# Two slabs side by side behind each norm, factors moved to the copy out of the banks, and products for two tiles

## The reference, cut to what matters

```python
mod = silu(c) @ w_mod + b_mod
sh1, sc1, g1, sh2, sc2, g2 = split(mod, 6)
h = rmsnorm(x, attn_norm_g) * (1 + sc1) + sh1        # "h4"
proj = h @ w_in                                      # 1856 columns: qa (1024), ka, cq, ckv
...                                                  # two kinds of attention
x = x + g1 * (mix @ w_out)
h = rmsnorm(x, mlp_norm_g) * (1 + sc2) + sh2         # "h6"
u = relu(h @ w_ff1)                                  # 8192 columns
x = x + g2 * ((u * u) @ w_ff2)
return rmsnorm(x, final_norm_g)
```

## Time and profile before

| | |
|---|---|
| median of 3 runs | 2221.35 us (2219.59 to 2227.68) |
| the profiled execution | 2218.01 us |
| its span in the trace | 2216.2 us |
| granted TensorE clock, mean | 0.988 |
| busy: PE / DVE / ACT | 2136.4 / 1507.9 / 1056.5 us |
| the last product before the first norm; the first behind it | 1207.70; 1214.86 us |
| the first two slabs behind the first norm end | 1248.58 us |
| the last product before the second norm; the first behind it | 1486.16; 1493.01 us |
| the first two slabs behind the second norm end | 1525.5 us |

### The profile page before, as it was taken

How to read it: one execution, slowest core, us unless ns; L and a number is a source line. 1 busy time by engine, 2 the same in 40 slices (tenths; PEclk the granted TensorE clock), 3 DMA queues, 4 the chain that set the end, 5 groups by cost and what they waited for, 6 DMA issues and landing times. The chain is left out here.

```text
span 2216.2 us, 29175 instructions
## 1 busy us (share of the span) xinstructions
PE 2136.4 (96%) x11414; PEld 1841.3 (83%) x11414; DVE 1507.9 (68%) x1919; ACT 1056.5 (48%) x1501; POOL 50.5 (2%) x51
## 2 busy tenths in 40 slices
PE   6999999999999999999998799998999999999998
PEld 5888888888888888888877698877888888888886
DVE  5967676789798777978955566556655566556655
ACT  4644554454444434444444556545443344334443
POOL 3200000000000000000000000000000000000000
PEclk9999999999999999999999999999999999999999
DMA  7787333779698897878955324354555555555553
GB/s 259 281 298 258 131 134 115 268 286 335 249 337 308 295 350 271 335 270 320 336 205 200 131 89 145 134 209 152 190 190 193 190 190 189 192 198 191 189 181 131
DMA packets 71047, 494.44 MB, mean 223 GB/s; under 512 B 8090, under 2 KB 8394, under 8 KB 13184
## 3 DMA queue, kind: packets, MB, share of 16 engines
q1 hardware_dynamic: 67968, 480.54, 60.0%
q0 software_dynamic: 2368, 11.32, 1.5%
q10 hardware_dynamic: 576, 0.73, 0.1%
HBM read 490.40 MB, written 2.16 MB: 222 GB/s over the span
## 5 line engine op out<-in xcount | busy, mean ns | idle before, releaser
L1657 DVE TENSOR_TENSOR m_WLO<-m_RAW,m_WHI 128x1024 fp32r<-128x1024 f32 (+1 forms) x728 | 880.9, 1222 | 539.4 <-ACT m_WHI L1329 527.2
L1329 ACT ACTIVATE m_WHI<-m_RAW 128x1024 fp32r<-128x1024 f32 (+1 forms) x728 | 753.8, 1045 | 748.3 <-PE region L974 388.2
L918 PE MATMUL region<-m_HL,m_WHI 128*128 128x512 f32 x1568 | 385.3, 396 | 1.4 <-ACT m_vw L1258 1.4
L974 PE MATMUL region<-m_WHI,m_HL 128*128 128x512 f32 x1152 | 361.8, 395 | 1.2 <-DVE m_HL L1845 0.5
L918 PEld LDWEIGHTS region<-m_HL,m_WHI 128*128 128x128 f32 x1568 | 289.3, 190 | 57.4 <-ACT m_vw L1258 1.8
L918 PE MATMUL region<-m_H,m_WHI 128*128 128x512 f32 x1376 | 332.6, 393 | 0.0
L918 PEld LDWEIGHTS region<-m_H,m_WHI 128*128 128x128 f32 x1376 | 254.6, 190 | 49.4
L974 PEld LDWEIGHTS region<-m_WHI,m_HL 128*128 128x128 f32 x1152 | 212.2, 188 | 43.3 <-issue 1.4
L974 PE MATMUL region<-m_WLO,m_HL 128*128 128x512 f32 x576 | 224.7, 390 | 0.0
L1710 DVE SCALAR_TENSOR_TENSOR m_ACC<-m_RAW,m_cact,m_ACC 128x2048 f32<-128x2048 f32 x90 | 211.2, 2346 | 1.8 <-DMA m_RAW<-in_w_mod 1.8
L922 PE MATMUL region<-m_HL,m_WLO 128*128 128x256 f32 x1568 | 208.8, 285 | 0.1
(11 more groups left out here) (296 smaller groups left out, 1787.5 us busy)
## 6 DMA issues: line engine op xcount, KB each, us to landing
m_RAW<-in_w_ff SPq DMA_DIRECT2D x128, 1024.0 KB, 4.8
m_RAW<-in_w_mod SPq DMA_DIRECT2D x96, 1024.0 KB, 5.8
m_RAW<-in_ffn_w_in SPq DMA_DIRECT2D x88, 1024.0 KB, 6.0
m_RAW<-in_ffn_w_out SPq DMA_DIRECT2D x44, 1024.0 KB, 6.4
m_RAW<-in_nsa_w_in SPq DMA_DIRECT2D x40, 1024.0 KB, 5.6
m_RAW<-in_nsa_w_out SPq DMA_DIRECT2D x16, 1024.0 KB, 5.0
m_RAW<-in_w_out SPq DMA_DIRECT2D x16, 1024.0 KB, 4.9
m_RAW<-in_w_in SPq DMA_DIRECT2D x10, 1024.0 KB, 4.7
```

The source lines that it names most:

```text
L918: mm = e.matmul(region[s["reg"]][:, b, :], hi[:, i, c:c + 128], both[:, k + a + i, :, :].rearrange("p a s -> p (a s)"), start=k + a + i == ...
L974: mm = e.matmul(o, lhs, rhs, start=start and i == 0, stop=fin and i == 2, skip_group_check=True)
L1329: e.activation(WHI[u % 4][:, 0:(z - a) * ncol], raw[:, a * ncol:z * ncol], ACT.Copy).then_inc(a_hi, 1)
L1657: e.tensor_tensor(WLO[u % 4][:, 0:m], raw[:, a * ncol:z * ncol], WHI[u % 4][:, 0:m].bitcast(F32), ALU.subtract).then_inc(v_lo, 1)
```

## The change

1. **Two slabs side by side.** qa 0 and qa 1, and relu 0 and relu 1, get chunks of four k tiles (`per=4`, 512 KB, parts of two k tiles: 128 x 512) and are queued alternately: four k tiles of the first (A), the same four of the second (B), the next four of A, and so on. Neither is `by_part` now.
2. **When the norms are put.** `x_ready` puts norms 0 to 3 before k tile 0 of A, and then two at a time: 4 and 5 before A's k tile 2, 6 and 7 before B's k tile 2, 8 and 9 before A's k tile 6, 10 and 11 before B's k tile 6, and so on.
3. **Factors at the copy out.** ACT's copies from banks 4 and 5 to `XGT` become four of 128 x 256 with the factor as scale, where there were two of 128 x 512. The factors are computed when their columns of `mod` are there (unit `factors`).
4. **Products for two tiles.** `HT = XGT * root` is now a `tensor_tensor`, for tiles 0 and 1 one at a time with the root read from bank 6, and from tile 2 on for two tiles at once (128 x 512) from `rstd`. ACT's copy of the root (`rowkeep`) stands behind norm 1, its copy of the last four turned tiles (`turnout`) behind norm 3. Of the unit norm 2, `LO[1]` comes before the product.
5. The four `final` units are put at every third tick, with a rate of one.

```diff
-    for s in (sl_qa[0], sl_qa[1], sl_ka, sl_qa[2], sl_qa[3], sl_cq, sl_ckv):
+    queue(sl_qa[0], sl_qa[1])
+    for s in (sl_ka, sl_qa[2], sl_qa[3], sl_cq, sl_ckv):
         queue(s)
...
+        if pi == 0:
+            queue(up[0], up[1])
+        for s in up[2 if pi == 0 else 0:]:
             queue(s)
...
-            s["by_part"] = s["x"] in seen
+            s["by_part"] = s["x"] in seen and s["list"][0][2] == 8
...
+            if p in (1, 4):
+                put("factors", p // 4)
...
-            while normed[x] < min(KT, k + 9):
+            c, second = k // 4 * 4, s["arg"] == 1
+            while normed[x] < (min(KT, c + 4 + 2 * second + (2 if k % 4 >= 2 else 0)) if s["arg"] < 2 else KT):
                 put("norm", x, normed[x])
                 normed[x] += 1
+                if normed[x] == 2:
+                    put("rowkeep", 2 if x == "h4" else 3)
+                if normed[x] == 4:
+                    put("turnout", x, 12)
...
-        put("turnout", which, 12)
         st["owed"] = 2
...
-    side.extend(("final", m0) for m0 in range(0, KT, 4))
+    for m0 in range(0, KT, 4):
+        side.extend([None, None, ("final", m0)])
+    st["rate"] = 1
...
-                    for b in range(2):
-                        e.activation(XGT[:, m0 + 2 * b:m0 + 2 * b + 2, :], two(bank[4 + b]), ACT.Copy).then_inc(b_out[4 + b], 1)
-            elif name == "rowcast":
+                    w.wait_ge(v_gates, 1 if which == "h4" else 2)
+                    g = G1c if which == "h4" else G2c
+                    for i in range(4):
+                        m = m0 + i
+                        ins = e.activation(XGT[:, m, :], two(bank[4 + i // 2])[:, i % 2, :], ACT.Copy, scale=g[:, m:m + 1])
+                        if i % 2:
+                            ins.then_inc(b_out[4 + i // 2], 1)
+            elif name == "rowkeep":
                 r, = arg
                 w.wait_ge(p_row, r)
+                if r > 1:
+                    w.wait_ge(v_ht, product_no("h4" if r == 2 else "h6", 1))
                 e.activation(rstd[:, :], bank[6][:, 0:S], ACT.Copy).then_inc(b_out[6], 1)
...
-                e.scalar_tensor_tensor(HT[m % 8 // 4][:, m % 4, :], XGT[:, m, :], g[:, m:m + 1], rstd[:, :],
-                                       ALU.mult, ALU.mult).then_inc(v_ht, 1)
-                if m > 0:
+                if m == 1 or m % 2 == 0:
+                    n = 1 if m < 2 else 2
+                    r = 2 if x == "h4" else 3
+                    root = by_token(rstd, n)
+                    if m == 2:
+                        low(1)
+                    if m < 2:
+                        w.wait_ge(p_row, r)
+                        root = bank[6][:, 0:S].rearrange("p (m s) -> p m s", m=1)
+                    else:
+                        w.wait_ge(b_out[6], filled(("rowcast", r), 6))
+                    w.wait_ge(b_out[4 + m % 4 // 2], filled(("xturn", x, m // 4 * 4), 4 + m % 4 // 2))
+                    if m >= 8:
+                        w.wait_ge(a_norm, base + m - 6)
+                        w.wait_ge(v_norm, base + m - 6)
+                    e.tensor_tensor(HT[m % 8 // 4][:, m % 4:m % 4 + n, :], XGT[:, m:m + n, :], root,
+                                    ALU.mult).then_inc(v_ht, 1)
+                if m > 0 and m != 2:
                     low(m - 1)
```

More of the change, by code:

```diff
@@ L182, in make_plan @@
     W = "w_in_2"
-    sl_qa = [slab("qa", i, W, 0, KT, 256 * i, 256, WIDE, "h4") for i in range(2)]
+    sl_qa = [slab("qa", i, W, 0, KT, 256 * i, 256, WIDE, "h4", per=4) for i in range(2)]
     sl_ka = slab("ka", 0, W, 0, KT, 1024, 256, [("f", 0, 0, 0, S), ("f", 128, 0, 256, S)], "h4")
@@ L202, in make_plan @@
     for pi, (s0, n) in enumerate(((0, 12), (12, 10), (22, 10))):
-        up = [slab("relu", j, "w_ff1_2", 0, KT, 256 * (s0 + j), 256, WIDE, "h6") for j in range(n)]
+        up = [slab("relu", j, "w_ff1_2", 0, KT, 256 * (s0 + j), 256, WIDE, "h6", per=4 if s0 + j < 2 else None)
+              for j in range(n)]
         for j, s in enumerate(up):
             s["hid"] = 22 + s0 + j
+        if pi == 0:
+            queue(up[0], up[1])
+        for s in up[2 if pi == 0 else 0:]:
             queue(s)
@@ L258, in unit @@
             have["row"] = u[1]
+            if u[1] == 1:
+                put("rowkeep", 1)
         if u == ("rstd", 0):
@@ L1174, in quarter, with product_no @@
         return v_x, name_slab("out1" if which == "h3" else "out2", m0)["x0"] + h + 1
+    def product_no(x, m):
+        return (m + 1 if m < 2 else m // 2 + 2) + (9 if x == "h6" else 0)
     def turned_no(which, m0):
@@ L1509, in scalar_program @@
                 x, m = arg
-                n = m + (1 if x == "h4" else 17)
-                w.wait_ge(v_ht, n)
+                w.wait_ge(v_ht, product_no(x, m))
                 w.wait_ge(p_part, P.ffn1_end if x == "h4" else P.out2_end)
@@ L1877, in vector_program @@
                 r, = arg
-                if r == 2:
-                    w.wait_ge(v_mod, 6)
-                    e.scalar_tensor_tensor(G1c[:, :], mod[:, 16:32], 1.0, g_att2, ALU.add, ALU.mult).then_inc(v_gates, 1)
-                    e.scalar_tensor_tensor(G2c[:, :], mod[:, 64:80], 1.0, g_mlp2, ALU.add, ALU.mult).then_inc(v_gates, 1)
                 w.wait_ge(a_sumsq, {1: 8, 2: 24, 3: 32}[r])
@@ L1917, in vector_program @@
                 ins.then_inc(v_sinks, 1)
+            elif name == "factors":
+                i, = arg
+                w.wait_ge(v_mod, (2, 5)[i])
+                g, c, own = ((G1c, 16, g_att2), (G2c, 64, g_mlp2))[i]
+                e.scalar_tensor_tensor(g[:, :], mod[:, c:c + 16], 1.0, own, ALU.add, ALU.mult).then_inc(v_gates, 1)
             elif name == "norm":
                 x, m = arg
-                base, g, sh = (0, G1c, 0) if x == "h4" else (16, G2c, 48)
+                base, sh = (0, 0) if x == "h4" else (16, 48)
                 def low(k):
@@ L1927, in vector_program @@
                 if x == "h4":
-                    w.wait_ge(v_gates, 2)
                     w.wait_ge(a_hid, 22)
@@ L1934, in vector_program @@
                     w.wait_ge(p_values, 32)
-                w.wait_ge(b_out[6], filled(("rowcast", 2 if x == "h4" else 3), 6))
-                w.wait_ge(b_out[4 + m % 4 // 2], filled(("xturn", x, m // 4 * 4), 4 + m % 4 // 2))
-                if m >= 8:
-                    w.wait_ge(a_norm, base + m - 7)
-                    w.wait_ge(v_norm, base + m - 7)
-                e.scalar_tensor_tensor(HT[m % 8 // 4][:, m % 4, :], XGT[:, m, :], g[:, m:m + 1], rstd[:, :],
-                                       ALU.mult, ALU.mult).then_inc(v_ht, 1)
-                if m > 0:
+                if m == 1 or m % 2 == 0:
[16 more added lines that the diff above has]
+                if m > 0 and m != 2:
                     low(m - 1)
@@ L2041, in gpsimd_program @@
             elif name == "qrzero":
-                w.wait_ge(v_ht, 16)
+                w.wait_ge(v_ht, product_no("h4", 15))
                 e.dma_start(cosT[:, :], A["c_cos"]).then_inc(l_rope, 16)
```

## The result

The changed kernel takes 2223.86 us (median of 20 runs, 2220.43 to 2228.22), the kernel before 2219.61 us beside it (median of 20 runs, 2216.16 to 2227.68). The ratio is 1.0016, interval 1.0009 to 1.0022: 2.0 to 4.9 us slower. That is clear of the noise of 20 runs, and within the 0.5% that the prediction called no change. The profiled execution took 2223.18 us.

The account below looks back on a forecast made before the run. PE, busy 96% of the span, bounds the kernel, so only its pauses and low clock could be won. 2218.0 - 2.2 + 2.8 = 2218.6 us for the profiled execution; with 3.3 for the median, about 2222, range 2211 to 2230.

Parts of the forecast that it names:

- as forecast: Whole kernel: waits in the places named, 0 to 3 more clock falls a norm, 2218 to 2229 us; chance 0.72.
- The gap: From root to first product at each norm: DVE and the high part start earlier, 0.7 us won each time.
- The first wait: Before A's tile 3, low part queued behind two splits and a double product: 2.5 us, 2.1 with the lower bound.
- The loops: Before A's tiles 7 and 11, low parts queued behind splits that wait for PE: 2.02 us each, per norm.
- The small waits: Before A's tiles 5, 9 and 13, PE waits 0.63 us each, per norm.
- The clock: In the two slabs, one further fall to low clock per norm, 1.4 us each, +2.8 us in all.
- The bound for falls: Limits on further clock falls at the norms: none (0), or three each (+8.4 us).
- HAM oscillation: Rival: repeated pauses keep PE's clock low through the two slabs, +12.0 and +13.2 us, 2246 us; chance 0.06.
- What was to cost nothing: Scaled copies, half-size splits (1.2 us more on DVE a norm, repaid by products) and half-size transfers: no added time.
- That the order does what it is for: Rival: DVE's splits run ahead unheld by PE, only the first low-clock stretch stays, -19.6 us, 2202 us; chance 0.08.
- its half: Rival: each loop shorter by 1 us or so through quicker hand-overs, 2210 to 2213 us; chance 0.11.
- The split waits for PE by its buffer, in any case: Argument that DVE's splits in the merged slabs cannot run ahead of PE, against the 2202 us rival.

Follow-up runs that it names:

- the experiments with the order: Changed kernel with norms put one tile earlier (2209.36 us), also with the last turned tiles copied behind norm 9 (2207.4 us), or two tiles earlier (2208.69 us).
- The first two experiments: New norm in the slab order of before, 2217.4 us; then merged slabs with the norm's products and copies of before, 2220.13 us.
- the merged slabs alone: Kernel before with alternating chunks of four k tiles and the change's norm and final places, but old products, factors and copies: 2220.13 us, ratio 0.9998.
- the new norm alone: Changed kernel with slabs one after another and norms nine tiles ahead as before, keeping factors at copy out and double products: 2217.4 us, ratio 0.9984.
- The late `turnout`: Changed kernel with only the copy of the last four turned tiles moved from behind norm 3 to behind norm 9: 2221.87 us, ratio 1.0004.
- PE kept busy: Changed kernel plus 18 unread wide products per norm, behind A's k tiles 2, 6 and 10, where PE waits: 2220.22 us, ratio 0.9999.
- five tiles instead of four: Changed kernel with the norms put one tile earlier at every place, turned-tile copy still behind norm 3: 2209.36 us, ratio 0.9954.
- the late copies: Changed kernel with norms one tile earlier and the copy of the last four turned tiles behind norm 9: 2207.4 us, ratio 0.9944.
- the kernels with the loops: The changed kernel (2223.86 us), the merged order with the old norm (2220.13 us), and the change with turned tiles copied behind norm 9 (2221.87 us).
- the best version: Changed kernel with norms one tile earlier and turned tiles copied behind norm 9: 2207.4 us, or 2207.09 us with the final copies also moved.

## Why the prediction was right, and what in it was off

**The time.** 2222 was forecast, from 2211 to 2230, and 2223.86 came. The case "as forecast" is the one that happened, and the experiments with the order show its mechanism. That the number fits to 2 us is in part luck. The sum forecast a difference of +0.6 us (-2.2 + 2.8), and +4.2 came. To it the prediction added 3.3 us, the distance of the median of three runs of the kernel before from its profiled execution; over 20 runs that distance is 1.6 us, and the same sum would have given 2220.2.

**The gap**, -0.7 us at each norm: -0.57 and -0.96, counted from the last product before the norm. The first two experiments show which half makes it: the merged slabs alone leave it at 7.16 / 6.85, the new norm alone has 6.42 / 6.06.

**The first wait**, 2.5 us with 2.1 as the lower bound: 2.12 and 2.42. A scaled copy out of a bank takes what was taken for it; the groups by form over the first norm:

```profile
L1483 ACT ACTIVATE m_XGT<-bank,m_G1c 128x256 f32<-128x256 f32 x4 | 1.5, 464 | 0.0
L1975 DVE TENSOR_TENSOR m_HT<-m_XGT,m_rstd 128x512 f32<-128x512 f32 x7 | 4.8, 685 | 0.0
L1682 DVE TENSOR_TENSOR m_WLO<-m_RAW,m_WHI 128x512 fp32r<-128x512 f32 x14 | 9.5, 692 | 9.3 <-ACT m_WHI L1348 7.7 <-PE region L979 1.4
```

464 ns against the 0.47 us taken, 685 against 0.69, 692 against 0.69. The late `turnout` shows that the copies set this wait: it falls to 0.68 / 1.01.

**The loops**, 2 x 2.02 at tiles 7 and 11: 1.95 twice, and 1.94 and 1.96. This is the step on which the sign hung, and it held to 0.08 us. The small waits, 3 x 0.63: 0.54 and 0.80, 0.44 and 0.21, and before tile 13 none. Slower work of PE ahead of a wait shortens it, and a fall of the clock lay there: behind tile 11 PE went through B's tiles 9 to 11 or 8 to 10 at the low clock. The other traces bear this out: without a fall there the wait before tile 13 stands, 0.54 and 0.58 us with PE kept busy and 0.54 at the first norm with the late `turnout`. At that kernel's second norm a fall ended with B's tile 9, before the stretch that counts for tile 13 begins, and the wait is again 0.54. All waits: 7.4 and 7.0 us, forecast 9.0 and 8.4.

**The clock** is the term that was mis-sized. One further fall for each norm, 1.4 us each, was counted; one came at the first norm and three at the second. Two slabs were to take 33.35 + 1.4 = 34.75 and 32.15 + 1.4 = 33.55 us, and took 34.68 and 36.98. At the second norm, 36.98 less 22.27 of pairs at full clock and 6.97 of waits leaves 7.7 us, where the forecast had 1.45 + 1.4: 21 slow pairs of 0.29 us more are 6.1 of it, and the rest lies at the edges of the five pauses, some 0.2 to 0.3 us each, which the waits in brackets leave out. At the first norm the fit to 0.07 us is luck: the waits came out 1.6 us shorter than forecast, and slow pairs and edges 1.6 us longer (5.05 against 3.45). The run with PE kept busy shortens the second norm's slabs by 3.5 us, the first's by 0.7 and the medians by 3.6, so one fall costs 1.1 us net, less than the 1.4 counted; it was their number that was too low. The bound for falls (three each, +8.4) held it. The Trainium skill (TensorE: Matmul & The Clock Gate, section HAM oscillation) was weighed as a rival; the trace of before had shown falls only behind pauses of 2.2 us and more, and here they came from 1.80 us on. Its picture of an array that falls back at each turn of the loop is what the second norm shows, a fall behind each of the three long pauses (1500.3 to 1524.0 us), and not what the first shows, one fall behind three. The price at the second norm is 3.5 us and not that of a clock that stays low, since each fall ends after some 3.2 us.

**What was to cost nothing** did cost nothing. The profile of the changed kernel names no wait of PE for a transfer or for POOL in the merged slabs. The eight more splits cost DVE what was said, and DVE's busy time in all is 1507.3 us against 1507.9. The prediction set the fixed cost of the Trainium skill (VectorE: DVE Perf Modes, section TRN2 errata) against the rows, 0.5 us against 1.2. The same section says that 58 cycles are too few and puts the measured fixed term near 150; by that the eight splits are 1.25 us, an estimate, and page and rows agree.

**The rivals.** That the order does what it is for was given 2202 us and 0.19 with its half. It did not happen, but the place in which it failed was one tile: with five tiles instead of four the kernel takes 2209.4, with the late copies 2207.4, between the half's 2210 and the whole's 2202. "The split waits for PE by its buffer, in any case" was the argument against it. The splits go on waiting in these kernels too; what one tile further takes away is the work that PE wants behind them. The price of the half does not follow from its condition: each of four loops shorter by 1 us, and no further fall, is 4 + 2.8 us and gives 2215, not 2210 to 2213.

**What stays open**: why the kernels with the loops have more falls at the second norm than at the first (3 against 1, 2 against 0, 2 against 0, one trace each) behind pauses that are alike (1.95, 1.95 against 1.94, 1.96 us in the change); and the wait of 1.8 us that is left in the best version, of which the `final` copies are argued to make 1.1.

## What to carry to other kernels

In a queue that is served in order, write down for each piece of work that the bound engine will want next what stands ahead of it, and which of that waits for the bound engine itself. Such a loop sets a pause for each turn (here 1.95 us, four times) although no engine but PE is loaded to the full, and one place earlier in the list can take it away: this was worth 14 us where the new norm by itself, with fewer products and its copies moved, was worth 3.5. Keep the distance at which work is prepared when you repair one place: one part less ahead, carried on through the rest of the kernel, cost 40 us.

## What was not expected of the hardware

- The stage between the norms ran in 237.6, 241.8 and 242.7 us in three kernels with one and the same order of work there. The granted clock from 1345 to 1385 us was 1.00 before the change, 0.91 after it, and 0.87 to 0.96 in the others; the work in that window is shifted by up to some 8 us between them.
- 18 products at each norm whose results nobody reads made the kernel 3.6 us faster.
- Equal pauses did not do equal things to the clock: 1.95 us passed once without a fall and once with one, within 9 us of each other, behind the first norm.
